# Sample attention by quads: four sequences per softmax tile, column tiles of 32, pages in two shared buffers

## The chip, the core and the metric

The kernel runs on one core of a Trainium2 chip. The time is the device time of one launch in microseconds (us), the median of several runs. Engines are named as the profile names them: PE (TensorE matmul), PEld (its weight load), DVE (VectorE), ACT (ScalarE), POOL (GpSimd), SP (SyncE, which here only issues DMAs and waits).

## What is computed

Two layers of a hybrid decoder, for a prompt of 1024 positions and for 8 short sample sequences of 4 positions each, 512 positions into their history. The change touches one part of layer 1, the sparse attention of the samples, whose keys and values lie in pages of 128 positions:

```python
def dsa_sample(q, k, v, qi, ki, wi, *, layer, cache_k, cache_v, cache_kidx, page_table):
    ...
    idx = index_select(qi, wi, ki_all, pos_q, k_sel)      # 129 of 516 keys per query
    ...
    ks = jnp.where(in_past, cache_k[layer, phys, off], k[nidx, nnew])
    vs = jnp.where(in_past, cache_v[layer, phys, off], v[nidx, nnew])
    return sparse_attend(q, ks, vs, idx, pos_q)

def sparse_attend(q, ks, vs, idx, pos_q):
    logits = jnp.einsum('nthd,ntkhd->nthk', q, ks).astype(jnp.float32) * ATT_SCALE
    ...
    p = jax.nn.softmax(jnp.where(valid, logits, -jnp.inf), axis=-1).astype(q.dtype)
    return jnp.einsum('nthk,ntkhd->nthd', p, vs)
```

The kernel does not gather keys. It computes the logits against all 512 paged keys and the 32 new ones (544 in all) and adds a large negative bias to those that were not chosen.

## The kernel before, in words

All dense work is a chain of 400 **slabs**. A slab is a block of a weight matrix with 128 output columns; SP loads it into one of three buffers (`load_slab`, which waits until the slab three places back has been multiplied), ACT writes its rounded part (L1064, `WH`), POOL the rest (L1531, `WL`), and PE multiplies 8 chunks of depth by three products each (L652, L653, L655). The result goes into one of two sets of PSUM banks, which ACT or DVE must empty before the slab after next may start (`evac_done`).

Every engine has its own hand-written program. It goes from slab to slab, and at the middle and at the end of each slab it calls its own `beside(n, end)`, which holds the side work due at that point. The engines run in program order, so side work that waits holds up all that stands behind it on its engine. F1A = 240 is the first slab of the stretch in question: the feed-forward part of layer 1 for the first half of the prompt (512 columns). Slabs 256 to 267 are up-projections in pairs (ACT copies the banks at L1204 and L1207, DVE does two convolution taps at L1823 and L1825 and, on the second of a pair, a product at L1949, after ACT's Silu at L1215). Slabs 268 to 275 are down-projections with 6 chunks of depth (DVE adds the banks to Z at L1864). Of the first two, PE computes four chunks each, then waits for the last `HLA` (L1937) of slab 267.

Beside these slabs run three things.

- Selection for the prompt, on DVE: at the end of each of slabs 256 to 271 three (in the last two: two) units of `best`, each a MAX8 pair (L2145) or a MATCH_REPLACE8 pair (L2143).
- A bisection for the last two prompt blocks, `threshold(k)` on DVE and `signs_of(k)` on ACT, in turns: DVE proposes a value (L2186 to L2191), ACT counts signs over 896 and 1024 columns (L1259), DVE takes the count and proposes the next. It has three steps per pair of up slabs and one per down slab.
- Sample attention, one sequence s for every two slabs. With a = n - 256: at the end of slab a = 2s PE computes `sample_logits(s)` (L843: four matmuls of 32 x 512 and four of 32 x 32, all float32; L844: the bias in bfloat16). DVE takes the row maximum (`sample_max`, L2252), ACT the exponential (L1271), DVE the reciprocal (`sample_recip`, L2257), ACT the scaling (L1276). At the end of slab a = 2s + 1 PE turns the probabilities (L853) and ACT copies them (`spt`, L1282 and L1283). At the end of slab a = 2s + 2 PE multiplies them by the values (`sample_values`, L864 and L865), and then does the logits of sequence s + 1. After each four sequences ACT keeps the sums (`kept`, L1288), PE turns them (L871), and ACT picks each head's own part (`atts`, L1295).

Keys have one buffer (`KP`), values another (`VP`). SP issues the four pages of a set one by one, each after reading its page number; the next keys once the logits of s are done, the next values once the value product of s is done. A set of either is 4 x 256 KB. From slab 275 on the same places hold the prompt's attention for its second half (logits at L896).

Of the kernel before, what the change touches and what calls it, by code (L numbers as in the profile page):

```python
# [22 lines left out]
I8 = mybir.dt.int8  # L23
# [142 lines left out]

def sample_at(n):

    a = n - F1A - S_FIRST
    return [[x // 2] if x % 2 == 0 and 0 <= x // 2 < SEQS else [] for x in (a - 1, a - 2, a)]  # L170

def kept_at(n):

    a = n - F1A - S_FIRST
    return [g for g in range(2) if a == 8 * g + 8], [g for g in range(2) if a == 8 * g + 9]
# [12 lines left out]
def build(nc, io):  # L189
    with ExitStack() as ctx:  # L190
# [53 lines left out]
        def piece(base, m):  # L244
# [87 lines left out]
            ("nmx", [P, 2], F32), ("psm", [P, 2], F32), ("prc", [P, 2], F32), ("rep", [NS, SEQS, NS], BF16),  # L332
# [20 lines left out]
        (spt, signs6), e = region(piece(z_off, 1), ("spt", [P, 5, NS], F32), ("signs6", [P, 7 * P], I8))  # L353
        assert e <= piece(z_off, 2)
        atts = at("atts", [P, 4, NS], F32, piece(z_off, 2))
# [4 lines left out]
        QBs = [at(f"QBs{c}", [P, SEQS, NS], F32, piece(z_off, 5 + c // 2) + c % 2 * SEQS * NS * 4) for c in range(4)]  # L360
# [84 lines left out]

        def dots_of(t):

            n = P * (3 + t // 8)
            return PS[:, (1, 3)[t % 2], 0:n] if t < 16 else pair(2 + t % 2, n)
# [8 lines left out]
        def attended_bank(p):  # L458
# [51 lines left out]
        k_in, v_in = sem("key_pages_in"), sem("value_pages_in")  # L510
        qb_zero, qb_set = sem("qb_cleared"), sem("qb_set")
        slg, smax, sexp, ssump, snorm, stp, ste, spv, satt = (
            sem("sa_" + n) for n in ("logits", "max", "exp", "rsum", "probs", "turned", "probs_turned", "values", "out"))
# [70 lines left out]
        def _(sp):  # L584
# [24 lines left out]
            def key_pages(s):  # L609
                for g in range(PAGES):  # L610
                    pg = page(s, g)
                    sp.dma_start(KP[:, :, HALF + g * PAGE:HALF + (g + 1) * PAGE],
                                 io["ck"][bass.ds(pg, 1)].rearrange("a p c s -> p (a c) s")).then_inc(k_in, 16)

            def value_pages(s):
                for g in range(PAGES):
                    pg = page(s, g)
                    sp.dma_start(VP[:, g, HALF:2 * HALF],
                                 io["cv"][bass.ds(pg, 1)].rearrange("a p c -> p (a c)")).then_inc(v_in, 16)

            for n in range(3, STEPS):
# [11 lines left out]
                if n == F1A + S_FIRST - 2:  # L633
# [3 lines left out]
                    value_pages(0)  # L637
# [10 lines left out]
        def _(pe):  # L648
# [180 lines left out]
            def sample_logits(s):  # L829
                if s == 0:  # L830
                    pe.wait_ge(qb_set, 8)
                    pe.wait_ge(sb_set, 2)
                    pe.wait_ge(rep_in, 16)
                    pe.wait_ge(ssc_set, 2)
                    pe.wait_ge(dot_relu, 48)
                else:
                    pe.wait_ge(sexp, s)
                pe.wait_ge(k_in, 64 * (s + 1))
# [8 lines left out]
            def sample_turn(s):  # L847
                pe.wait_ge(snorm, s + 1)
                if s >= 1:
                    pe.wait_ge(ste, 2 * s)  # L850
                for t in range(5):
                    w = P if t < 4 else NS
# [1654 lines left out]
```

## Time and profile before

| | us |
|---|---|
| median of 3 runs | 2792.41 |
| lowest, highest | 2786.95, 2792.7 |
| the profiled execution, its time | 2798.2 |
| its span, first to last instruction | 2796.5 |
| PE busy in the span | 2593.8 (93%) |
| DVE, ACT, POOL busy | 1479.6, 1264.8, 1213.7 |
| from the end of slab 256 (the first sample logits) to the first prompt logits of slab 275 | 1753.5 to 1967.9, that is 214.4 |

The last row is the stretch in which the sample attention runs. An engine's idle time is given with what ended it: [1.62 <-PE PS L844] behind a row means that the engine was idle for 1.62 us until the matmul of line 844 had finished.

### The profile page before, as it was taken

The page shows a single profiled execution, that of the slowest core. Times are in us where ns is not written, and L with a number is a line of the kernel's source. Part 1 is how long each engine was busy: PE and PEld are TensorE (multiplying, and loading weights), DVE is VectorE, ACT ScalarE, POOL GpSimd, SP SyncE. Part 2 cuts the span into 40 slices and gives each one's busy share as a digit, 9 for nine tenths or more (in the row PEclk, how much of TensorE's full clock was granted, in tenths as well). Part 3 has the DMA queues.
Part 4 walks back from the last instruction along what each step waited for, and adds up shares of the span by engine and source line. Part 5 has one row for each costly group of instructions (what it writes and reads, how often), then busy time and mean ns, then how long its engine had stood idle before and what let it go on. Part 6 is the DMA issues. An engine that isn't in the chain of part 4 may idle for free. (4 is left out here: it accounts for less than half of the span.)

```text
span 2796.5 us, 39511 instructions
## 1 busy us (share of the span) xinstructions
PE 2593.8 (93%) x15720; PEld 2221.3 (79%) x15720; DVE 1479.6 (53%) x2271; ACT 1264.8 (45%) x2019; POOL 1213.7 (43%) x1030
## 2 busy tenths in 40 slices
PE   7989999999999999999998976987999988999997
PEld 7989887888897788999987854543666667999997
DVE  2342476332574587634577488775553445542435
ACT  3111354343453444445443464673895734332333
POOL 2212455454464843434456664221332335454443
PEclk9999999999999999999999988998999998999998
DMA  3101222222313222222223313332212122222222
GB/s 127 43 32 46 84 90 83 91 94 95 98 63 110 83 76 68 69 76 69 89 91 119 110 59 115 110 123 91 68 57 89 57 89 84 84 87 87 84 94 80
DMA packets 96099, 235.45 MB, mean 84 GB/s; under 512 B 10443, under 2 KB 31499, under 8 KB 95531
## 3 DMA queue, kind: packets, MB, share of 16 engines
q1 hardware_dynamic: 85344, 210.95, 23.8%
q10 hardware_dynamic: 10570, 21.97, 2.2%
q8 instruction: 125, 2.05, 0.3%
q14 instruction: 60, 0.48, 0.1%
HBM read 219.43 MB, written 13.45 MB: 83 GB/s over the span
## 5 line engine op out<-in xcount | busy, mean ns | idle before, releaser
L1531 POOL TENSOR_TENSOR WL<-RAW,WH 128x1024 fp32r<-128x1024 f32 (+2 forms) x400 | 888.9, 2222 | 1479.7 <-ACT WH L1064 1479.2
L652 PE MATMUL PS<-XH,WH 128*128 128x272 f32 (+2 forms) x3312 | 1061.5, 331 | 38.1 <-DVE XL L1747 13.6
L653 PE MATMUL PS<-XL,WH 128*128 128x272 f32 (+2 forms) x3312 | 1045.3, 326 | 0.0
L655 PE MATMUL PS<-XH,WL 128*128 128x272 f32 (+2 forms) x3312 | 874.6, 326 | 0.0
L652 PEld LDWEIGHTS PS<-XH,WH 128*128 128x128 f32 x3312 | 630.7, 190 | 101.3 <-issue 39.0
L1064 ACT ACTIVATE WH<-RAW 128x1024 fp32r<-128x1024 f32 (+2 forms) x400 | 388.3, 971 | 611.9 <-DMA RAW<-in_slabs 593.7
L653 PEld LDWEIGHTS PS<-XL,WH 128*128 128x128 f32 x3312 | 630.5, 190 | 39.9 <-issue 1.0
L655 PEld LDWEIGHTS PS<-XH,WL 128*128 128x128 f32 x3312 | 561.6, 190 | 41.5
L652 PE MATMUL PS<-HH,WH 128*128 128x272 f32 (+1 forms) x880 | 265.2, 316 | 15.5 <-DVE HL L1937 13.8
L653 PE MATMUL PS<-HL,WH 128*128 128x272 f32 (+1 forms) x880 | 262.1, 312 | 0.0
L655 PE MATMUL PS<-HH,WL 128*128 128x272 f32 (+1 forms) x880 | 217.3, 312 | 0.0
L1864 DVE TENSOR_TENSOR Z<-Z,PS 128x512 f32<-128x512 f32 (+1 forms) x96 | 67.6, 704 | 236.8 <-PE PS L655 235.9
L652 PEld LDWEIGHTS PS<-HH,WH 128*128 128x128 f32 x880 | 168.5, 191 | 27.8 <-DVE HL L1937 14.9
L1823 DVE SCALAR_TENSOR_TENSOR cvB<-extB,fpar,cvB 128x560 f32<-128x560 f32 (+1 forms) x132 | 106.6, 808 | 149.5 <-ACT cvB L1207 146.4
L1816 DVE TENSOR_SCALAR cvB<-extB,fpar 128x560 f32<-128x560 f32 x88 | 54.3, 617 | 248.3 <-POOL extB L1650 178.9
L1204 ACT ACTIVATE extB<-PS 128x240 f32<-128x240 f32 (+3 forms) x308 | 92.1, 362 | 184.7 <-PE PS L655 184.7
L653 PEld LDWEIGHTS PS<-HL,WH 128*128 128x128 f32 x880 | 168.4, 191 | 8.0
L655 PEld LDWEIGHTS PS<-HH,WL 128*128 128x128 f32 x880 | 146.4, 191 | 7.5
L1823 DVE SCALAR_TENSOR_TENSOR cvA<-extA,fpar,cvA 128x512 f32<-128x512 f32 x44 | 58.3, 1324 | 129.2 <-ACT cvA L1207 127.4
L1825 DVE SCALAR_TENSOR_TENSOR cvB<-extB,fpar,cvB 128x560 f32<-128x560 f32 (+1 forms) x132 | 123.8, 938 | 4.7
L1575 POOL TENSOR_TENSOR Z<-Z,sqb 128x512 f32<-128x512 f32 (+1 forms) x64 | 98.2, 1551 | 14.2 <-ACT sqb L1133 14.2
L652 PE MATMUL PS<-HHA,WH 128*128 128x512 f32 x176 | 76.6, 435 | 27.3 <-DVE HLA L1937 15.6
(326 smaller groups left out, 3322.8 us busy)
## 6 DMA issues: line engine op xcount, KB each, us to landing
RAW<-in_slabs SPq DMA_DIRECT2D x272, 512.0 KB, 3.5
RAW<-in_slabs SPq DMA_DIRECT2D x96, 384.0 KB, 3.0
RAW<-in_slabs SPq DMA_DIRECT2D x32, 256.0 KB, 2.6
KP<-in_ck SPq DMA_DIRECT2D x32, 256.0 KB, 3.2
VP<-in_cv SPq DMA_DIRECT2D x32, 256.0 KB, 3.0
xb_rows<-spill ACTq DMA_DIRECT2D x8, 272.0 KB, 4.4
Z<-xb_rows ACTq DMA_DIRECT2D x1, 2176.0 KB, 9.2
out_o_y<-Z ACTq DMA_DIRECT2D x4, 544.0 KB, 2.8
```

The source lines that it names most:

```text
L652: pe.matmul(o, WH[n % 3][:, k, :], hi(k)[:, c], start=first, stop=False)
L653: pe.matmul(o, WH[n % 3][:, k, :], lo(k)[:, c], start=False, stop=False)
L655: mm = pe.matmul(o, WL[n % 3][:, k, :], hi(k)[:, c], start=False, stop=last)
L1064: act.activation(WH[n % 3][:, 0:kc, :], RAW[n % 3][:, 0:kc, :], ACT.Copy).then_inc(w_hi, 1)
L1204: ins = act.activation(dst, src_, ACT.Copy)
L1531: pool.tensor_tensor(WL[n % 3][:, 0:kc, :], RAW[n % 3][:, 0:kc, :], WH[n % 3][:, 0:kc, :].bitcast(F32), ALU.subtract).then_inc(w_lo, 1)
L1575: pool.tensor_tensor(z, z, LNS[q][3][:, :], ALU.subtract).then_inc(ln_sub, 1)
L1816: dve.tensor_scalar(out, row[:, 2:2 + w], taps_w[2], taps_w[3], ALU.mult, ALU.add).then_inc(tap_sem, 1)
L1823: dve.scalar_tensor_tensor(out, row[:, 0:w], taps_w[0], out, ALU.mult, ALU.add).then_inc(tap_sem, 1)
L1825: dve.scalar_tensor_tensor(out, row[:, 1:1 + w], taps_w[1], out, ALU.mult, ALU.add).then_inc(done, 1)
L1864: dve.tensor_tensor(by_bank(z, gr), by_bank(z, gr), slot(n), ALU.add).then_inc(evac_done[n % 2], 1)
```

## The change

The eight sequences form two quads, g = 0 and 1. In a quad the 128 rows of one softmax tile are 4 chunks of features (c, two heads each, 32 partitions) by 4 sequences (8 rows each).

- **Logits.** Sequence s comes at the end of slab a = s, one per slab. Chunk c multiplies only its own 32 partitions of the tile: four matmuls of 32 x 512 and four of 32 x 32 that write to partitions 0, 32, 64 and 96. The queries of a sequence stand in 8 of the 32 columns, the others are zero, so the four sequences of a quad add up in one pair of banks. The bias is added once for a quad, on all 128 partitions.
- **Softmax.** Maximum, exponential, reciprocal and scaling come once for a quad (slabs a = 3 and 7), on 128 x 544. They are turned at a = 4 and a = 11.
- **Values.** Sequence s comes at the end of slab a = 8 + s: 16 matmuls of 32 x 128 and 4 more for the new values, again in four column groups.
- **Pages.** `KP` and `VP` both serve keys and values; the set for step a + 2 is issued after step a.
- **`rep`**, the small matrix that spreads the bias, is loaded in 8 pieces instead of 1, on ACT's queue, at the point where the input projection of layer 1 begins (slab 128).

```diff
 def sample_at(n):
     a = n - F1A - S_FIRST
-    return [[x // 2] if x % 2 == 0 and 0 <= x // 2 < SEQS else [] for x in (a - 1, a - 2, a)]
+    return ([g for g in range(2) if a == (QUAD, 2 * SEQS - QUAD - 1)[g]], [a - SEQS] if SEQS <= a < 2 * SEQS else [],
+            [a] if 0 <= a < SEQS else [], [g for g in range(2) if a == QUAD * g + QUAD - 1])
...
                 a = n - 3 - F1A - S_FIRST
-                if a % 2 == 0 and 0 <= a // 2 < SEQS - 1:
-                    sp.wait_ge(slg, a // 2 + 1)
-                    key_pages(a // 2 + 1)
-                if a % 2 == 1 and 0 <= a // 2 - 1 < SEQS - 1:
-                    sp.wait_ge(spv, a // 2)
-                    value_pages(a // 2)
+                if 0 <= a < SEQS:
+                    sp.wait_ge(slg, a + 1)
+                    (key_pages if a + 2 < SEQS else value_pages)((a + 2) % SEQS)
+                elif SEQS <= a < 2 * SEQS - 2:
+                    sp.wait_ge(spv, a - SEQS + 1)
+                    value_pages(a - SEQS + 2)
...
             def sample_logits(s):
...
-                both = pair(3, SK, NS)
-                for o, keys, bias in ((both[:, 0:PAST], lambda c: KP[:, c, HALF:2 * HALF], sbias[:, 0:PAST]),
-                                      (both[:, PAST:SK], lambda c: K[:, c, NP:NT], sbias[:, PAST:SK])):
+                both = pair(3 - g, SK)
+                at0 = P * g + 24 * x
+                for cols in (slice(0, PAST), slice(PAST, SK)):
                     for c in range(4):
-                        pe.matmul(o, QBs[c][:, s, :], keys(c), start=(c == 0), stop=False)
-                    mm = pe.matmul(o, rep[:, s, :], bias, start=False, stop=True)
+                        keys = pages_of(s)[:, c, HALF:2 * HALF] if cols.start == 0 else K[:, c, NP:NT]
+                        mm = pe.matmul(both[32 * c:32 * c + 32, cols], QBs[c][:, at0:at0 + 32], keys, start=(x == 0), stop=False)
                 mm.then_inc(slg, 1)
+                if x == QUAD - 1:
+                    for cols in (slice(0, PAST), slice(PAST, SK)):
+                        mm = pe.matmul(both[:, cols], rep[:, g, :], sbias[:, cols], start=False, stop=True)
+                    mm.then_inc(sbiased, 1)
...
             def sample_values(s):
-                pe.wait_ge(ste, 2 * (s + 1))
-                pe.wait_ge(v_in, 64 * (s + 1))
...
+                pe.wait_ge(ste, 2 * (g + 1))
+                pe.wait_ge(page_in[s % 2], 64 * (s // 2 + 5))
                 for t in range(4):
-                    pe.matmul(o, spt[:, t, :], VP[:, t, HALF:2 * HALF], start=(t == 0), stop=False)
-                pe.matmul(o, spt[0:NS, 4, :], VS[:, :], start=False, stop=True).then_inc(spv, 1)
+                    for c in range(4):
+                        pe.matmul(sample_bank(g)[32 * c:32 * c + 32, x * P:(x + 1) * P], spt[:, t, 32 * c:32 * c + 32],
+                                  pages_of(s)[:, t, HALF + c * P:HALF + (c + 1) * P], start=(t == 0), stop=False)
...
-            def sample_max(s):
-                j = s % 2
-                dve.wait_ge(slg, s + 1)
-                dve.tensor_reduce(nmx[0:NS, j:j + 1], pair(3, SK, NS), AXX, ALU.max, negate=True).then_inc(smax, 1)
+            def sample_max(g):
+                dve.wait_ge(sbiased, g + 1)
+                dve.tensor_reduce(nmx[:, g:g + 1], pair(3 - g, SK), AXX, ALU.max, negate=True).then_inc(smax, 1)
```

On DVE, at the end of slab 258, before the change (cvA are the taps, HLA is the rest of the hidden row, SC the scores of the selection, tk the small values of the bisection):

```order
L1823 SCALAR_TENSOR_TENSOR cvA_159<-extA_157,fpar_178,cvA_159 128x512
L1825 SCALAR_TENSOR_TENSOR cvA_159<-extA_157,fpar_178,cvA_159 128x512
L1937 TENSOR_TENSOR HLA_153<-hfA,HHA_164 128x512
L2252 TENSOR_REDUCE nmx<-PS 32x1
L2257 RECIPROCAL prc<-psm 32x1
L2145 MAX m8a<-SC_149 128x8
L2145 MAX m8b<-SC_149 128x8
```

and after it:

```order
L1851 SCALAR_TENSOR_TENSOR cvA_159<-extA_157,fpar_178,cvA_159 128x512
L1853 SCALAR_TENSOR_TENSOR cvA_159<-extA_157,fpar_178,cvA_159 128x512
L1965 TENSOR_TENSOR HLA_153<-hfA,HHA_164 128x512
L2173 MAX m8a<-SC_149 128x8
L2173 MAX m8b<-SC_149 128x8
L2171 MATCH_REPLACE SC_149<-m8a,SC_149 128x640
```

The maximum and the reciprocal are gone from here; DVE's program now holds them twice (after L1977 of slabs 259 and 263, as 128x1) instead of eight times.

On PE, between slabs 258 and 259, before the change (VP, KP are the pages, QBs the queries, VS and K the new values and keys, rep and sbias the bias):

```order
L864 MATMUL PS<-VP,spt 32x512 x4
L865 MATMUL PS<-VS,spt 32x512
L843 MATMUL PS<-KP,QBs_214 32x512
L843 MATMUL PS<-KP,QBs_215 32x512
L843 MATMUL PS<-KP,QBs_216 32x512
L843 MATMUL PS<-KP,QBs_217 32x512
L844 MATMUL PS<-sbias,rep 32x512
L843 MATMUL PS<-K,QBs_214 32x32
```

After it, the logits between slabs 257 and 258, and the values between slabs 264 and 265:

```order
L860 MATMUL PS<-VP,QBs_215 32x512
L860 MATMUL PS<-VP,QBs_216 32x512
L860 MATMUL PS<-VP,QBs_217 32x512
L860 MATMUL PS<-VP,QBs_218 32x512
L860 MATMUL PS<-K,QBs_215 32x32
L860 MATMUL PS<-K,QBs_216 32x32
L860 MATMUL PS<-K,QBs_217 32x32
L860 MATMUL PS<-K,QBs_218 32x32
...
L881 MATMUL PS<-KP,spt 32x128 x16
L884 MATMUL PS<-VS,sptn 32x128 x4
```

A value product and a logits product no longer stand at the same place: the first eight slabs carry logits alone, the next eight values alone.

## Rows read from the trace of the kernel before

**Rows 1.** Busy time by stretch: length, PE, PEld, DVE, ACT, POOL, clock, DMA share, GB/s

```profile
1700.00:1753.00 53.00, 33.07 (x104) 24.39 (x105) 49.62 (x107) 24.45 (x38) 17.63 (x11) 0.77 0.44 142
1753.50:1967.90 214.40, 184.77 (x673) 97.90 (x673) 135.80 (x276) 129.55 (x225) 43.65 (x31) 0.93 0.35 109
1778.50:1803.10 24.60, 22.54 (x82) 11.69 (x81) 17.41 (x37) 16.80 (x28) 5.45 (x4) 0.93 0.41 128
```

**Rows 2.** Who waited for whom on DVE, 1753.5 to 1968: total, times, longest

```profile
DVE tk L2186 <- ACT signs L1259: 28.6, 8, 9.3
DVE nmx L2252 <- PE PS L844: 25.8, 6, 10.5
DVE cvA L1823 <- ACT cvA L1207: 9.0, 6, 1.5
DVE prc L2257 <- ACT sp L1271: 6.9, 8, 0.9
```

**Rows 3.** DVE in order of time, one pair of up slabs: start, duration, what

```profile
1783.00 0.71 DVE L2252 TENSOR_REDUCE nmx<-PS 32x1 f32<-32x544 f32 x1 [1.62 <-PE PS L844]
1784.58 0.15 DVE L2257 RECIPROCAL prc<-psm 32x1 f32<-32x1 f32 x1 [0.86 <-ACT sp L1271]
...
1789.55 0.13 DVE L2186 TENSOR_TENSOR tk<-tk 128x2 uint32<-128x2 f32 x1
...
1792.66 0.16 DVE L2186 TENSOR_TENSOR tk<-tk 128x2 uint32<-128x2 f32 x1 [2.58 <-ACT signs L1259]
...
1807.62 0.71 DVE L2252 TENSOR_REDUCE nmx<-PS 32x1 f32<-32x544 f32 x1 [1.61 <-PE PS L844]
```

**Rows 4.** PE in order of time, the sample work of one pair

```profile
1772.33 5.32 PE L864 MATMUL PS<-VP,spt 128*32 128x512 f32 x8 [2.45 <-ACT spt L1283]
1777.57 1.04 PE L865 MATMUL PS<-VS,spt 32*32 32x512 f32 x2
1778.54 3.62 PE L843 MATMUL PS<-KP,QBs 128*32 128x512 f32 x8
...
1782.41 0.44 PE L843 MATMUL PS<-K,QBs 128*32 128x32 f32 x8
...
1782.89 0.50 PE L652 MATMUL PS<-XH,WH 128*128 128x512 f32 x1
...
1788.66 0.46 PE L853 MATMUL PS<-ident,sp 32*128 32x32 f32 x5
```

**Rows 5.** DVE in order of time, slabs 271 and 272

```profile
1943.31 0.69 DVE L1864 TENSOR_TENSOR Z<-Z,PS 128x512 f32<-128x512 f32 x1
...
1947.22 2.05 DVE L2149 TENSOR_SCALAR MB<-SC 128x640 bf16<-128x640 f32 x2
1949.19 0.15 DVE L2186 TENSOR_TENSOR tk<-tk 128x2 uint32<-128x2 f32 x1
...
1959.87 0.16 DVE L2186 TENSOR_TENSOR tk<-tk 128x2 uint32<-128x2 f32 x1 [9.30 <-ACT signs L1259]
```

**Rows 6.** PE in order of time: prompt values, two column halves (128*64) side by side

```profile
2194.70 1.97 PE L927 MATMUL PS<-PTB,VT 128*64 128x128 f32 x32
```

**Rows 7.** All instructions on the value pages: duration min/median/max in ns, first and last start

```profile
L864 PEld LDWEIGHTS PS<-VP,spt x64: 106/111/178, 1772.3 to 1954.9; 128*32 128x32 f32 x64
```

**Rows 8.** The page, section 6: DMA issues, KB each, us to landing

```profile
RAW<-in_slabs SPq DMA_DIRECT2D x272, 512.0 KB, 3.5
...
KP<-in_ck SPq DMA_DIRECT2D x32, 256.0 KB, 3.2
```

**Rows 9.** SP's queue in order of time: one set of key pages

```profile
1783.71 4.46 SPq L612 DMA_DIRECT2D KP<-in_ck  x4
```

**Rows 10.** ACT and its DMA queue in order of time, around slab 128

```profile
852.93 0.45 ACTq L1489 DMA_DIRECT2D rep<-in_rep  x1
...
853.91 1.06 ACT L1064 ACTIVATE WH<-RAW 128x1024 fp32r<-128x1024 f32 x1 [2.97 <-DMA RAW<-in_slabs]
...
859.75 1.06 ACT L1064 ACTIVATE WH<-RAW 128x1024 fp32r<-128x1024 f32 x1 [2.84 <-DMA RAW<-in_slabs]
```

More of the change, by code:

```diff
@@ L359, in build @@
         signs = (signs6, signs7)
-        QBs = [at(f"QBs{c}", [P, SEQS, NS], F32, piece(z_off, 5 + c // 2) + c % 2 * SEQS * NS * 4) for c in range(4)]
+        QBs = [at(f"QBs{c}", [P, SEQS * NS], F32, piece(z_off, 5 + c // 2) + c % 2 * SEQS * NS * 4) for c in range(4)]
         PRB = at("PRB", [P, NP], F32, T0 - 4 * WID[1] * 4)
@@ L509, in build @@
         counted, proposed, small, placed = (sem("t_" + n) for n in ("counted", "proposed", "settled", "places"))
-        k_in, v_in = sem("key_pages_in"), sem("value_pages_in")
+        page_in = [sem("pages_in0"), sem("pages_in1")]
         qb_zero, qb_set = sem("qb_cleared"), sem("qb_set")
-        slg, smax, sexp, ssump, snorm, stp, ste, spv, satt = (
-            sem("sa_" + n) for n in ("logits", "max", "exp", "rsum", "probs", "turned", "probs_turned", "values", "out"))
+        slg, sbiased, smax, sexp, ssump, snorm, stp, ste, spv, satt = (
+            sem("sa_" + n) for n in ("logits", "biased", "max", "exp", "rsum", "probs", "turned", "probs_turned", "values", "out"))
         lg, amax, aexp, asum, anorm, atp, ate, apv, ao_hi, ao_lo = (
@@ L867, in sample_values_turn @@
             def sample_values_turn(g):
                 pe.wait_ge(sv_kept, g + 1)
-                for c in range(4):
-                    mm = pe.transpose(PS[:, 1, c * P:(c + 1) * P], kept[:, c * P:(c + 1) * P], ident[:, :])
+                own = ident[:, :].rearrange("p (c r) -> p c r", c=4)
+                for x in range(QUAD):
+                    mm = pe.matmul(sample_bank(g)[:, x * NS:(x + 1) * NS].rearrange("p (c r) -> p c r", c=4),
+                                   kept[:, x * P:(x + 1) * P], own[:, :, 8 * x:8 * x + 8], start=True, stop=True)
@@ L985, in beside @@
                 if end:
-                    late, out, now = sample_at(n)
-                    for s in late:
-                        sample_turn(s)
+                    late, out, now, _ = sample_at(n)
+                    for g in late:
+                        sample_turn(g)
                     for s in out:
@@ L1360, in beside @@
                 if end:
-                    late, out, now = sample_at(n)
-                    for s in late:
-                        sample_turned(s)
+                    late, _, _, full = sample_at(n)
+                    for g in late:
+                        sample_turned(g)
                     done, back = kept_at(n)
@@ L1368, in beside @@
                         sample_out(g)
-                    for s in now:
-                        sample_exp(s)
-                        sample_norm(s)
+                    for g in full:
+                        sample_exp(g)
+                        sample_norm(g)
                     for q in NORM_PLAIN:
@@ L1488, in _ @@
             act.dma_start(identb[:, :], io["identb"]).then_inc(identb_in, 16)
-            act.dma_start(rep[:, :, :], io["rep"]).then_inc(rep_in, 16)
+            for g in range(2):
+                for x in range(QUAD):
+                    act.dma_start(rep[:, g, :].rearrange("p (c s r) -> p c s r", c=4, s=QUAD)[:, :, x, :],
+                                  io["rep"][:, QUAD * g + x, :].rearrange("p (c r) -> p c r", c=4)).then_inc(rep_in, 16)
             act.dma_start(fpar1[:, :, :], io["fpar"][1]).then_inc(fpar_in, 16)
```

115 lines of the change are left out of this document (62 added, 53 removed).

## The prediction, made before the changed kernel was run

> **What bounds the kernel now.** I read the table of busy time by stretch first, then the waits of DVE, then the order of time. PE is 93% busy over the whole span, which says that most of the kernel is bound by it. The stretch of the sample attention is different. It lasts 214.4 us [rows 1], from the first sample logits to the first prompt logits of slab 275. PE is busy for 184.8 of it, but with the sample's own products, and it is not what the next step always waits for. DVE is busy for 135.8 and spends most of the rest in four waits [rows 2]: 28.6 for ACT's sign counts (the bisection, one after another by nature), 25.8 for the sample logits, 9.0 for ACT's copies, 6.9 for ACT's exponential. 135.8 + 70.3 = 206.1 of 214.4; the rest is small gaps. So DVE's program, its own work plus what it waits for in turn, accounts for the stretch, and I price the change on DVE first and ask afterwards whether PE keeps up.
>
> One pair of up slabs shows it [rows 3]. From one sample maximum to the next are 1807.62 - 1783.00 = 24.6 us. Of these the sample takes 1.61 (wait for the logits) + 0.71 (maximum) + 0.86 (wait for the exponential) + 0.15 (reciprocal) = 3.3. Everything else, 21.3, is selection (from the reciprocal to the next bisection step, 1784.73 to 1789.55, three units in 4.8), the bisection with a wait of 2.58, taps and the product. None of that changes.
>
> **Part 1, DVE's sample steps.** Removed: the wait for logits, 25.8 over six of the eight sequences; the wait for the exponential, 6.9; eight times 0.71 + 0.15, 6.9. Together 39.6 [rows 2, 3]. Added: two quads with the same steps, on 128 partitions instead of 32. I take the same durations, as the columns stay 544, and no wait for logits, as PE is far ahead there (part 3): 2 x (0.71 + 0.86 + 0.15) = 3.4. If the first exponential also had to wait for something of ACT, up to 2 us each more. Net -36.2.
>
> **Part 2, the end of the sample work.** At slab 272 DVE waits 9.30 for a sign count [rows 5], because ACT's program has the copy of the last value sums ahead of that count, and the value product came late. In an ordinary turn of the bisection that wait is 2.58 [rows 3]. With the last value product one slab earlier and a third as long, I expect the ordinary wait: -6.7. It could stay halfway if ACT's eight head copies fall there: -4.
>
> **Part 3, can PE keep up?** A slab of the up part takes 1788.66 - 1782.89 = 5.8, one of six chunks 4.3 [rows 4]. The sample work per sequence before: logits 1782.89 - 1778.54 = 4.35, turn 0.46, values 1778.54 - 1772.33 = 6.2 at a mixed clock.
> A float32 matmul appears as two records. Logits have the same 8 records of 512 columns (3.62 / 8 = 0.45 each) and 8 short ones (0.44 together). One after the other that is 4.1, four abreast 1.3. Values have 40 records of 128 columns, a quarter of 0.45 each, 0.11: 4.5 one after the other, 1.1 four abreast. No row shows four column tiles. The nearest shows two: 32 records in 1.97, 0.062 each instead of 0.11 [rows 6], which gives 2.5. I take 2.0 for either, nearer to that row than to the ideal.
> In the up slabs PE then needs 2 x (5.8 + 2.0) = 15.6 per pair, DVE 21.3. With no overlap at all it is 20.6, still covered. So the gain on DVE doesn't depend on the tiles running abreast there.
> In slabs 268 to 271 PE has less cover. DVE needs 0.69 + 4.8 + 0.5 = 6.0 for each of the first two; 3.9 + 0.5 = 4.4 for slab 270, which has two units; and 1949.19 - 1943.31 + 0.5 = 6.4 for 271 [rows 3, 5]: 22.8. PE needs 4 x (4.3 + 2.0) + 0.5 for the turn = 25.7. That gives back 2.9; with no overlap (4.5) it gives back 12.9, with four abreast nothing. I add 2 for low-clock stretches after PE's waits at the switch to the down slabs.
>
> **Part 4, ACT.** It loses six exponentials, scalings and turned copies. It was idle anyway (129.6 busy of 214.4 [rows 1]), so 0. If this shortens its side of the bisection it is a gain of a few tenths per pair, which I leave in the range.
>
> **Part 5, pages.** The 16 sets are the same bytes, now one set per slab instead of one. SP needs 4.46 to issue a set and a page lands 3.2 after that [rows 8, 9]: 7.7. The set is issued two slabs ahead of its use, 12.6 to 15.6 us. The slab load behind it on SP's queue waits for a slab to be multiplied; a slab with its sample work takes 6.3 or more, and SP's queue is held for 4.46 + 0.34, so the load isn't late. The share of DMA time rises from 0.35 [rows 1] to about 0.43. Cost 0, with up to 2 us per late set as the outer bound. The second set before the stretch now stands behind a slab load instead of ahead of it; DVE is busy 49.6 of 53.0 there [rows 1], so 0.
>
> **Part 6, `rep` in eight pieces.** Seven more issues of 0.45 on ACT, 3.2 us [rows 10]. ACT's slab work at 853.91 moves to 857.1; the next one, at 859.75, waits 2.84 for its own slab. ACT absorbs it, and PE has two slabs of lead: 0, at most +2.
>
> **Sum.** -39.6 + 3.4 - 6.7 + 2.9 + 2.0 = -38.0. The stretch becomes 176.4. The profiled execution would take 2798.2 - 38.0 = 2760.2; it lay 5.8 above the median, so for the median 2792.4 - 38.0 = **2754.4 us**.
>
> **Rivals.**
> **(a) The four column tiles run one after the other**, so the change does not do what "side by side" says. Logits 4.1, values 4.5. The up slabs hide it; the down slabs give back 12.9 instead of 2.9: 2764. A lower clock in those slabs does the same and worse, up to 2776. For: no row has four. Against: two tiles do overlap [rows 6].
> **(b) Each weight load waits for the product ahead of it.** A load takes 0.11 [rows 7]. Then values take 40 x 0.22 = 8.8 and logits 5.4. The down slabs need 4 x 13.1 + 0.5 = 52.9 against 22.8, 30.1 more; two up pairs with values 29.2 against 21.3, four with logits 22.4, together 20.2, less PE's lead of two slabs, 11.6. 38.7 in all in place of the 2.9: about 2790. Against: in rows 6 each of 32 records has its own load and takes 0.062, less than the load alone.
 If a share x of PE's time ran at half speed, a pair would need 15.6 (1 + x). It loses against DVE's 21.3 only from x = 0.37, and all parts together eat the gain at x = 0.65. At x = 0.8: pairs 28.1, 6 x 6.8 = 41 less the lead of 11.6; down slabs 45.6 against 22.8; the last four slabs +13: 65 instead of 4.9, about 2814. Against: where PE has no slack it is busy, and there the clock was 0.93 on average [rows 1].
> **(d) More than forecast**, down to 2740: four abreast, and ACT's lighter load shortens the bisection.
>
> **Chances.** Forecast (2744 to 2762) 0.62; (a) with clock 0.19; (d) 0.05; (b) 0.06; (c) 0.05; something unnamed near no change 0.03. The range from 2740 to 2776 takes in the forecast, (a) and (d). A measurement of this kernel tells about 0.2% from no change, 5.6 us. Faster than that 0.89, within it 0.06, slower 0.05.
>
> **What would show it.** Right: DVE has two waits for logits instead of eight, near 0 each; the time between DVE's steps of two pairs is 21 us; the wait of 9.3 is gone; PE waits for DVE or for the banks in slabs 257 to 267. Wrong: logits over 3 us or values over 4 us per sequence; PE waiting for pages; a clock below 0.8 in the down slabs; the part after slab 275 longer than before.

## The result, and the profile after

The changed kernel takes 2757.1 us, median of 4 runs (2752.3 to 2760.9), against 2792.6 for the kernel before beside it (2787.0 to 2793.6): 0.987 of its time, 95% interval 0.985 to 0.989, 35.5 us less. The profiled execution took 2760.7, its span is 2759.0. The four runs lie in two pairs, at 2752.3 and 2753.5 and at 2760.7 and 2760.9, so a difference of a few us from 2757.1 says little unless a trace shows it too.

Line numbers move: the slab products are now L667 to L670, the sample logits L860, their values L881 and L884, the bisection's comparison L2214, the maximum L2279, the reciprocal L2283, ACT's exponential L1295, POOL's split L1559.

Busy time by stretch (length, PE, PEld, DVE, ACT, POOL, clock, DMA share, GB/s), from the first sample logits to the first prompt logits, and the last part of it:

```profile
1758.10:1929.90 171.80, 130.25 (x878) 94.94 (x877) 132.61 (x263) 108.79 (x185) 43.24 (x31) 0.87 0.45 136
1902.60:1929.90 27.30, 27.30 (x195) 21.18 (x187) 21.55 (x48) 20.34 (x38) 10.52 (x6) 1.00 0.42 130
```

The stretch went from 214.4 [rows 1] to 171.8 us, 42.6 less. PE works 54.5 less in it, DVE 3.2 less: the busier one of the two was cut, and now they are level. In this execution the kernel reaches the stretch 4.5 us later than the kernel before does, so the spans differ by 37.5 only, and the medians by 35.5. Most of that comes from far ahead of anything that was changed, from a lower granted clock between 300 and 400 us. Same columns, the kernel before and then the changed one:

```profile
300.00:400.00 100.00, 95.95 (x612) 86.41 (x611) 66.29 (x84) 40.88 (x54) 50.76 (x27) 0.98 0.26 84
```

```profile
300.00:400.00 100.00, 95.90 (x592) 86.33 (x591) 68.05 (x83) 39.60 (x52) 50.92 (x27) 0.93 0.26 84
```

In the run with `rep` in one transfer, below, the clock there is 0.98 too, and it reaches the stretch at 1753.9.

Who waited for whom in the stretch (total, times, longest), DVE, then PE, then POOL and ACT:

```profile
DVE tk L2214 <- ACT signs L1283: 21.4, 9, 2.6
DVE cvA L1851 <- ACT cvA L1231: 9.0, 6, 1.5
DVE prc L2283 <- ACT sp L1295: 1.7, 2, 0.9
```

```profile
PE PS L667 <- POOL WL L1559: 25.3, 6, 8.4
PE PS L872 <- ACT sp L1299: 12.9, 1, 12.9
PE PS L667 <- DVE HLA L1965: 3.4, 1, 3.4
```

```profile
POOL WL L1559 <- ACT WH L1088: 133.5, 19, 13.8
ACT signs L1283 <- DVEq L2275: 46.1, 15, 5.3
```

Against [rows 2] the 25.8 for logits are gone, the longest wait for a count is 2.6 instead of 9.3, and the exponential is waited for twice. PE now waits for POOL's splits, which wait for ACT's rounding, which stands behind ACT's sign counts, which wait for DVE's proposals (L2275).

PE in order of time, logits and then values of one sequence:

```profile
1771.77 1.06 PE L860 MATMUL PS<-KP,QBs 128*32 128x512 f32 x8
1772.65 0.24 PE L860 MATMUL PS<-K,QBs 128*32 128x32 f32 x8
...
1833.38 1.08 PE L881 MATMUL PS<-KP,spt 128*32 128x128 f32 x32
1834.39 0.42 PE L884 MATMUL PS<-VS,sptn 32*32 32x128 f32 x8
```

Logits take 1.3 us instead of 4.3, values 1.5 instead of 6.2 [rows 4]. The 6.2 were at a mixed clock; a value product of the kernel before that ran at the full one took 4.5 (1846.33 to 1850.86).

DVE's bisection steps serve as marks. Until slab 268 the durations between them repeat with every pair of slabs: 3.1 between two steps of one slab, then one to the next slab's end, then one to the middle of the slab after. Before they were 3.1, 10.4, 11.1 (24.6 a pair, one pair of the five 22.9); after they are 3.1, 10.4, 7.7 (21.3) in three pairs of five and 3.1, 13.5, 7.7 (24.3) in the two with a quad's softmax. The table gives five such pairs, from slab 258 on, and the rest up to the first prompt logits, for every run below (each step is timed at its copy under a mask, on DVE in order of time):

| kernel | five pairs, us | rest, us | median, us |
|---|---|---|---|
| before | 121.4 | 81.4 | 2792.5 |
| after | 112.6 | 50.4 | 2757.1 |
| softmax later, in the kernel before | 119.0 | 82.7 | 2792.4 |
| four groups, in the kernel before | 114.7 | 66.7 | 2770.5 |
| one group | 112.8 | 63.2 | 2768.7 |
| one buffer per kind | 112.7 | 62.9 | 2767.3 |
| quads alone (both) | 122.3 | 77.6 | 2792.9 |
| extra maximum | 116.9 | 48.1 | 2760.1 |
| quad's softmax later | 117.7 | 48.1 | 2757.4 |
| rep in one transfer | 112.6 | 51.9 | 2756.3 |
| fewer units in the up slabs | 107.3 | 53.7 | 2755.7 |
| units early and late | 99.0 | 53.1 | 2746.7 |
| units done by slab 273 | 99.0 | 52.7 | **2746.2** |
| more units early | 95.1 | 52.5 | 2750.6 |

Most of the gain, 31.0, lies in the rest; the pairs gave 8.8, and 2.8 the steps ahead of the first mark. Busy time in the rest, same columns as above, before and then after:

```profile
1886.50:1967.90 81.40, 64.19 (x216) 33.06 (x214) 38.11 (x83) 37.01 (x70) 14.45 (x9) 0.87 0.30 92
```

```profile
1879.50:1929.90 50.40, 41.44 (x299) 31.48 (x299) 36.81 (x79) 33.82 (x67) 14.74 (x9) 0.86 0.33 100
```

DVE's work in it is 1.3 less, PE's 22.8. The kernel before has three value and two logits products there, the changed one four of values.

### The profile page after: what moved, and what is told of

The parts are those of the page before. It is cut to its first block, busy times and chain, and to the rows that moved or that the text cites. A ratio compares the mean times of both kernels' runs of the same rounds, so it can differ in the third digit from the quotient of the medians.

```text
span 2759.0 us, 39856 instructions
## 1 busy us (share of the span) xinstructions
PE 2538.9 (92%) x15926; PEld 2219.2 (80%) x15926; DVE 1487.2 (54%) x2259; ACT 1245.5 (45%) x1981; POOL 1220.2 (44%) x1030
## 4 chain that ended last, share of the span: by engine, by line
PE 68%; DVE 16%; ACT 7%; issue 4%; DMA 2%; POOL 1%; ACTq 0%; SPq 0%; DVEq 0%; POOLq 0%
PE PS L667 21%; PE PS L668 20%; PE PS L670 20%; DMA RAW<-in_slabs 2%; DVE SC L2171 2%; POOL WL L1559 1%; PE PS L920 1%; ACT WH L1088 1%; DVE cvB L1853 1%; DVE cvB L1851 1%; DVE cvA L1851 1%; PE PS L951 1%; PE PS L839 1%; DVE m8b L2173 1%; PE PS L936 1%
## 5 line engine op out<-in xcount | busy, mean ns | idle before, releaser
L1559 POOL TENSOR_TENSOR WL<-RAW,WH 128x1024 fp32r<-128x1024 f32 (+2 forms) x400 | 889.8, 2225 | 1438.1 <-ACT WH L1088 1437.9
L667 PE MATMUL PS<-XH,WH 128*128 128x272 f32 (+2 forms) x3312 | 1064.7, 332 | 58.4 <-POOL WL L1559 22.1
L670 PE MATMUL PS<-XH,WL 128*128 128x272 f32 (+2 forms) x3312 | 875.7, 326 | 0.0
L667 PEld LDWEIGHTS PS<-XH,WH 128*128 128x128 f32 x3312 | 631.9, 191 | 123.1 <-issue 41.5
L670 PEld LDWEIGHTS PS<-XH,WL 128*128 128x128 f32 x3312 | 562.6, 191 | 42.0
L667 PE MATMUL PS<-HH,WH 128*128 128x272 f32 (+1 forms) x880 | 265.0, 316 | 16.5 <-DVE HL L1965 14.2
L670 PE MATMUL PS<-HH,WL 128*128 128x272 f32 (+1 forms) x880 | 216.8, 312 | 0.0
L1851 DVE SCALAR_TENSOR_TENSOR cvB<-extB,fpar,cvB 128x560 f32<-128x560 f32 (+1 forms) x132 | 112.6, 853 | 149.4 <-ACT cvB L1231 146.3
L667 PEld LDWEIGHTS PS<-HH,WH 128*128 128x128 f32 x880 | 168.3, 191 | 28.9 <-DVE HL L1965 15.3
L670 PEld LDWEIGHTS PS<-HH,WL 128*128 128x128 f32 x880 | 146.1, 191 | 7.4
L667 PE MATMUL PS<-HHA,WH 128*128 128x512 f32 x176 | 75.5, 429 | 32.6 <-DVE HLA L1965 15.8
```

The costliest lines, as they stand in the source:

```text
L667: pe.matmul(o, WH[n % 3][:, k, :], hi(k)[:, c], start=first, stop=False)
L670: mm = pe.matmul(o, WL[n % 3][:, k, :], hi(k)[:, c], start=False, stop=last)
L1559: pool.tensor_tensor(WL[n % 3][:, 0:kc, :], RAW[n % 3][:, 0:kc, :], WH[n % 3][:, 0:kc, :].bitcast(F32), ALU.subtract).then_inc(w_lo, 1)
L1851: dve.scalar_tensor_tensor(out, row[:, 0:w], taps_w[0], out, ALU.mult, ALU.add).then_inc(tap_sem, 1)
```

## Experiments

My theory at first was the prediction's: DVE sets the up slabs, its wait for logits was the loss, and PE matters in the down slabs alone. The rival: PE's saved work is the gain.

**One group of columns.** The products of all chunks go to group 0, so they can't run abreast; the bias goes to each group by itself. The attention of three chunks in four is left out, the matmuls of keys and values keep their number and shapes.

```diff
-mm = pe.matmul(both[32 * c:32 * c + 32, cols], QBs[c][:, at0:at0 + 32], keys, start=(x == 0), stop=False)
+mm = pe.matmul(both[0:32, cols], QBs[c][:, at0:at0 + 32], keys, start=(x == 0 and c == 0), stop=False)
...
-pe.matmul(sample_bank(g)[32 * c:32 * c + 32, x * P:(x + 1) * P], spt[:, t, 32 * c:32 * c + 32], ...
+pe.matmul(sample_bank(g)[0:32, x * P:(x + 1) * P], spt[:, t, 32 * c:32 * c + 32], ...
```

> The changed kernel with all four chunks' products of a sequence on one group of 32 columns instead of four, the number of matmuls and their shapes the same (the bias goes to the other three groups alone, and the attention of three chunks in four is lost, so the sample outputs are not those of the reference). With one group the products can't run beside each other: logits 8 x 0.45 + 0.44 = 4.1 us instead of 1.3, values 40 x 0.11 = 4.5 instead of 1.5. Theory (DVE's program sets the up slabs, PE only the down slabs): nothing in the up slabs, where PE is idle for 20 to 40 us; in the four down slabs with values 4 x 3.0 = 12, so 2757 + 12 = 2769. Rival (PE's saved time is the gain): 8 x (2.8 + 3.0) = 46 more, 2803, as slow as before or slower. Rival (the products ran beside each other for another reason than the groups): no change, 2757.

2768.7 (2766.5 to 2773.8), 11.5 us more, 0.992 of before (0.990 to 0.993). PE in order of time, the first logits and one set of values:

```profile
1754.41 3.59 PE L860 MATMUL PS<-KP,QBs 128*32 128x512 f32 x8 [0.17 <-issue]
...
1846.27 3.68 PE L882 MATMUL PS<-VP,spt 128*32 128x128 f32 x32
```

So the groups are what makes them run abreast: 1.06 against 3.59 for eight records, 1.08 against 3.68 for 32. The five pairs are untouched (112.8), the rest is 12.8 longer: as the theory says, and in a kernel that has two page buffers (see "quads alone").

**Softmax later, in the kernel before.** If DVE's wait for logits is the loss, it is enough to let DVE come later.

```diff
 # DVE, at the end of a slab
-for s in sample_at(n)[2]:
-    sample_max(s)
-    sample_recip(s)
 ...
 if (n, end) in STEP_AT:
     threshold(STEP_AT[n, end])
+if end:
+    for s in sample_at(n)[2]:
+        sample_max(s)
+        sample_recip(s)
 # ACT: sample_exp and sample_norm likewise, behind signs_of(k)
```

> The kernel before with one thing moved: DVE's maximum and reciprocal of a sequence stand behind the bisection step of the same slab end instead of ahead of the selection units (some 5 us later), and ACT's exponential behind the sign counts. No quads, no column groups, pages as before. Theory (a large part of the gain is DVE's 25.8 us wait for logits): the wait is gone, 2792.5 - 20 to 25 = 2770, less what PE's turn then waits for the probabilities. Rival (the gain is PE's saved work): PE's work is unchanged, so no change, 2792.

2792.4 (2789.2 to 2794.5), ratio 0.9998 (0.9988 to 1.0008): no change. Waits of DVE and then of PE in that kernel, 1753 to 1968:

```profile
DVE tk L2187 <- ACT signs L1259: 32.8, 9, 9.8
DVE nmx L2253 <- PE PS L844: 15.7, 2, 11.2
...
DVE Z L1865 <- PE PS L655: 5.2, 3, 2.7
```

```profile
PE PS L853 <- ACT sp L1276: 12.4, 7, 2.8
PE PS L864 <- DMA VP<-in_cv: 10.1, 3, 5.9
```

The wait for logits is left in two places, where it is long, and others have grown (counts 28.6 to 32.8, the add of a product 2.6 to 5.2). PE waits more (12.4 instead of 1.0 for the scaled probabilities). In the five pairs 2.4 us were won, and 1.3 lost again in the rest. My theory fell on this run: of the 25.8 us at most what lay in the up slabs, 1.6 a pair, was DVE's to gain; elsewhere the wait only showed that PE was late.
Following the chain of work back through one pair of up slabs of the kernel before (start, duration) shows what the 1.6 belonged to:

```profile
1783.00 0.72 DVE nmx L2252
...
1786.30 1.72 DVE SC L2143 x2
...
1791.21 1.41 ACT signs L1259 x3
...
1796.57 0.26 ACT spt L1282
...
1796.95 5.32 PE PS L864 x8
```

It is a ring: PE's values and logits (10.7 of the 24.6), then DVE's maximum, with ACT's exponential, its selection units and proposal (7.2), then ACT's sign counts, rounding, bank copies and at last `spt` (6.8), for which the next values wait [rows 4]. In two of the five pairs PE's wait ends otherwise, once with a value page and once with `atts`. No engine alone set these slabs. The ring gets shorter when the maximum comes later (pairs of 23.7 here) or when PE's products do ("four groups", below, 22.9), down to what DVE needs by itself, 21.3 and 1.7.

**Extra maximum.** One more reduction per slab, eight in all.

```diff
+for s in sample_at(n)[2]:
+    dve.tensor_reduce(s8[:, s:s + 1], ssc[:, :], AXX, ALU.max)
 for g in sample_at(n)[3]:
     sample_max(g)
```

> The changed kernel with one more reduction of 32 x 544 float32 on DVE at the end of each of the eight slabs with sample logits; its result is not used. Theory (DVE sets the up slabs): 8 x 0.7 = 5.6 us longer, 2763; each bisection step of slabs 258 to 265 comes 0.7 later per slab. Rival (PE or ACT sets them): no change, 2757.

2760.1 (2757.9 to 2765.0): 3.0 more, an interval that reaches from none to the expected 5.6. The trace is plainer: the durations are 11.0 and 8.3 instead of 10.4 and 7.7, 0.6 for each reduction, and five pairs, which hold seven of the eight, take 4.3 more. DVE does set the up slabs of the changed kernel. Then 2.3 come back. Same columns as the first table of stretches, the slab behind the last up slab in this kernel and in the changed one:

```profile
1893.00:1901.90 8.90, 7.45 (x103) 5.49 (x104) 6.78 (x14) 3.88 (x13) 0.00 (x0) 1.00 0.44 129
```

```profile
1892.10:1902.60 10.50, 9.05 (x97) 6.53 (x97) 6.79 (x15) 3.92 (x13) 0.00 (x0) 0.67 0.44 123
```

The same work takes 8.9 us at a clock of 1.00 and 10.5 at 0.67. In both PE idles much ahead of it; what decides which of them meets the low level there I can't tell from these runs.

**One buffer per kind.** Keys go to `KP`, values to `VP`, and a set is issued when the one before it has been used.

```diff
-    sp.wait_ge(slg, a + 1)
-    (key_pages if a + 2 < SEQS else value_pages)((a + 2) % SEQS)
+    sp.wait_ge(slg, a + 1)
+    key_pages(a + 1)
...
-    sp.wait_ge(spv, a - SEQS + 1)
-    value_pages(a - SEQS + 2)
+    sp.wait_ge(spv, a - SEQS + 1)
+    value_pages(a - SEQS + 1)
```

> The changed kernel with the page buffers as before: all key sets go to one, all value sets to the other, and a set is issued only when its predecessor has been used; one set per slab as in the changed kernel. A set needs 4.46 us of issue and 3.2 to land, 7.7. Theory: an up slab takes 11.4 us, so nothing there; from the first down slab on, where a slab takes 4.3 + 1.5 = 5.8, PE waits about 3 to 4 us for each of three value sets, and SP's slab loads stand behind them: 2757 + 11 = 2768. Rival (the second buffer is not needed, the pages are hidden anyway): 2757.

2767.3 (2762.8 to 2772.6), 10.2 more. PE's waits for pages:

```profile
PE PS L856 <- DMA KP<-in_ck: 11.6, 6, 2.5
PE PS L877 <- DMA VP<-in_cv: 10.4, 4, 4.9
```

The 11.6 for keys lie where PE has slack and cost nothing (112.7 for five pairs); the rest is 12.5 longer, with 9.6 of the waits for values in it. In the changed kernel PE doesn't wait for pages at all.

**Four groups, in the kernel before**, without quads. The sums of the four chunks are not put together; each product has the size of the changed kernel's.

```diff
-    for c in range(4):
-        pe.matmul(o, QBs[c][:, s, :], keys(c), start=(c == 0), stop=False)
+    for c in (1, 2, 3, 0):
+        pe.matmul(o(c), QBs[c][:, s, :], keys(c), start=True, stop=(c > 0))
...
-    pe.matmul(o, spt[:, t, :], VP[:, t, HALF:2 * HALF], start=(t == 0), stop=False)
+    for c in range(4):
+        pe.matmul(o(c), spt[:, t, :], VP[:, t, HALF + c * P:HALF + (c + 1) * P], start=(t == 0), stop=False)
```

> The kernel before with column groups alone: each chunk's logits and values of a sequence go to a group of 32 columns of its own, four abreast, values as 128-wide products; softmax per sequence, pages and schedule as before. The chunks' sums are not put together, so the sample attention is wrong, but each product has the size of the changed kernel. Theory after the first four runs (in the down slabs PE's own work and its wait for value pages set the pace, in the up slabs DVE): up pairs 24.6 - 1.6 = 23.0, five pairs, some 7 us; in the down slabs 3 to 4 sequences each 7.0 us of PE shorter, part of which goes into a longer wait for value pages (12.3 us now): 10 to 20 us. 2792.5 - 17 to 27 = 2766 to 2776. Rival (the gain needs the two softmax tiles): under 7 us, 2786 or more.

2770.5 (2767.6 to 2775.6), 0.993 of before (0.992 to 0.995): 21 of the 35 us, with one softmax per sequence. The pairs have 3.1, 10.4, 9.4: DVE's 21.3 and a softmax of 1.7, as expected, and no wait for logits in them. What holds PE now:

```profile
PE PS L866 <- ACT spt L1287: 17.7, 4, 5.2
PE PS L866 <- DMA VP<-in_cv: 9.4, 2, 6.0
```

**Quads alone**: the edits of "one group" and "one buffer per kind" together.

> The changed kernel with both of its other parts undone: all products of a sequence on one group of columns (the attention of three chunks in four is lost) and one page buffer per kind. What is left are the two softmax tiles, the schedule of eight logits and then eight values, and the values in 128-wide products. One part undone alone cost 11.5 (groups) and 10.2 us (buffers). Theory (in a down slab the page set, 7.7 us behind the last use, comes on top of the products that use it, 4.5): 12.2 a slab instead of 8.8 with two buffers, three times, so 10 on top of the 11.5: 2779, and the quads alone are worth about 14. Rival (the waits overlap, the longer product hides the pages): 2769.

2792.9 (2789.5 to 2796.0), ratio 1.0004 (0.9994 to 1.0013). All of the gain is gone, where I expected 22 of 36 us to go. All of PE's waits in the stretch but one of 0.2, and the chain followed back from 1875 to 1765, share of each line:

```profile
PE PS L856 <- DMA KP<-in_ck: 15.7, 7, 2.7
PE PS L878 <- DMA VP<-in_cv: 15.1, 6, 5.1
```

```profile
by line: PE PS L856 30.7%; DMA KP<-in_ck 21.5%; SPq L612 12.9%; SPq L623 10.4%; issue 8.0%; PE PS L878 6.6%; DMA VP<-in_cv 5.3%; SPq L629 2.4%; PE PS L663 1.9%; PE PS L881 1.8%; PE PS L666 1.7%; PE PS L664 1.7%; PE PS L861 0.3%
```

PE waits for no other engine, and the chain holds its products (L856 are the logits), the reading of page numbers and issuing of pages on SP (L612, L623, L629) and their landing, nothing of DVE or ACT. In the changed kernel the same view (it cuts the line off) is the reverse, DVE's program with ACT's counts and copies:

```profile
by line: DVE SC L2171 22.8%; DVE cvA L1851 11.7%; DVE m8b L2173 10.9%; DVE m8a L2173 10.0%; issue 7.2%; ACT signs L1283 6.6%; DVE cvA L1853 6.2%; ACT WH L1088 4.1%; DVE tk L2214 3.4%; DVE hfA L1977 3.1%; ACT cvA L1231 3.1%; DVE HLA L1965 2.
```

With that the four kernels with quads read as one rule:

| | two shared buffers | one per kind |
|---|---|---|
| four groups | 2757.1 | 2767.3 |
| one group | 2768.7 | 2792.9 |

Either part takes 24 to 26 us off 2792.9, the other one then 10 to 12 more. Each part of the stretch is as long as the longer of two paths, PE's with its pages and DVE's with its counts. The table of marks says where the second cut is lost. In the five pairs either cut alone brings PE's path below DVE's (122.3 to 112.8 or 112.7), and the other adds nothing (112.6). In the rest, where PE is the longer one, both count: 77.6, then 63.2 or 62.9, then 50.4.

**rep in one transfer.**

```diff
-for g in range(2):
-    for x in range(QUAD):
-        act.dma_start(rep[:, g, :].rearrange(...)[:, :, x, :], io["rep"][:, QUAD * g + x, :]...).then_inc(rep_in, 16)
+act.dma_start(rep[:, :, :], io["rep"]).then_inc(rep_in, 16)
```

> The changed kernel with the array rep laid out by the host in the order of its tile and loaded by one transfer instead of eight. Theory (seven more issues of 0.6 us on ACT are hidden): 2757, no change, though ACT's slab work after them comes 4 us earlier. Rival (they delay PE, the 5 us by which the changed kernel's trace lies behind at slab 140): 2752.

2756.3 (2753.8 to 2758.3): no change that can be told. In the changed kernel, on ACT and its queue in order of time:

```profile
857.80 4.79 ACTq L1516 DMA_DIRECT2D rep<-in_rep  x8
...
863.12 1.06 ACT L1088 ACTIVATE WH<-RAW 128x1024 fp32r<-128x1024 f32 x1 [7.30 <-issue]
```

ACT's next slab comes after 7.30 us of issuing, 4.79 of them for `rep`, and what reaches PE at the next product, at 866.71, is a wait of 0.21.

The 5 us by which that trace was behind aren't caused by the eight transfers: the median doesn't change, and the changed kernel is 4.9 behind the kernel before as soon as the first of them is issued (857.80 against 852.93 [rows 10]).

**Quad's softmax later**, in the changed kernel; the edit is that of "softmax later".

> The changed kernel with a quad's maximum and reciprocal on DVE behind the bisection step of its slab end, and its exponential on ACT behind the sign counts. In the changed kernel the three durations between bisection steps are 3.1, 10.4, 7.7 us in a pair of up slabs without a quad and 3.1, 13.5, 7.7 in one with: 3.1 more, of which 1.7 are the softmax steps and 1.5 a two-column comparison that takes 1.65 instead of 0.15 while POOL runs a split. Theory (DVE's first operation on two SBUF operands waits while POOL's split holds their common access, and whether it meets it is a matter of timing): the comparison takes 0.15 in these two pairs, a quad costs 1.7 to 2.5, the time is 1 to 3 us less, 2755. Rival (the 1.5 belong to the quad whatever the timing): 3.1 as before, 2757.

It rests on this row of the changed kernel, DVE and POOL in order of time:

```profile
1802.41 2.41 POOL L1559 TENSOR_TENSOR WL<-RAW,WH 128x1024 fp32r<-128x1024 f32 x1 [7.36 <-ACT WH L1088]
...
1803.19 1.65 DVE L2214 TENSOR_TENSOR tk<-tk 128x2 uint32<-128x2 f32 x1
```

A comparison of two columns takes 1.65 us and ends when POOL's split does (1804.8); elsewhere it takes 0.15. Moved, it takes 0.15 in both quads. But the time is 2757.4 (2756.0 to 2761.8), and a quad costs 5.7 instead of 3.1. DVE and POOL of this kernel:

```profile
1798.66 0.72 DVE L2280 TENSOR_REDUCE nmx<-PS 128x1 f32<-128x544 f32 x1
...
1802.23 2.36 POOL L1560 TENSOR_TENSOR WL<-RAW,WH 128x1024 fp32r<-128x1024 f32 x1 [10.75 <-ACT WH L1088]
1803.34 1.80 DVE L1852 SCALAR_TENSOR_TENSOR cvA<-extA,fpar,cvA 128x512 f32<-128x512 f32 x1 [2.92 <-ACT cvA L1231]
```

The split now holds a convolution tap (1.80 instead of 0.75), and DVE waits 2.92 for ACT, which does the exponential ahead of its copies: 1.7 + 2.9 + 1.05 = 5.7. So whom the split meets is timing, as the theory says; the gain I expected of it isn't there.
The Trainium skill (SBUF — State Buffer, "SBUF: two separate sides") says that a DVE operation with two SBUF inputs and a GpSimd operation that reads SBUF exclude each other for a whole instruction. These rows agree, down to an operation of two columns.

**Moving DVE's work.** If DVE sets the up slabs and PE the rest, selection units should leave the up slabs. Only the table of units per slab changes:

```diff
-TOP45 = dict(zip(list(range(F1A + 2, F1A + 8)) + list(range(F1A + 16, F1A + 32)), [3] * 20 + [2] * 2))
+# fewer in the up slabs: range(F1A + 16, F1A + 34), [3] * 6 + [3, 2] * 6 + [3, 3, 3, 3, 2, 2]
+# early and late:        range(F1A + 16, F1A + 34), [4] * 5 + [3] + [2] * 12 + [3, 3, 3, 3, 3, 2]
+# done by slab 273:      range(F1A + 16, F1A + 33), [4] * 6 + [2] * 12 + [4, 3, 3, 3, 3]
+# more early:            range(F1A + 16, F1A + 33), [5, 5, 5, 5, 4, 4] + [2, 2, 1] * 4 + [4, 3, 3, 3, 3]
```

> The changed kernel with six of DVE's selection units moved: 3 and 2 in turn instead of 3 in each of slabs 257 to 268, and 3, 3, 3, 3, 2, 2 in slabs 269 to 274 instead of 3, 3, 2, 2. Theory (DVE sets the up slabs, PE the down slabs): 6 x 1.6 = 9.6 us off the up slabs, pairs of 19.7 instead of 21.3, and 1 to 3 given back in slabs 271 to 274: 2750. Rival (PE's clock or POOL's splits set the up slabs now): no change, 2757.

2755.7 (2752.3 to 2759.3), 1.4 less where 7 were expected; too little to tell from no change. Pairs without a quad are 19.7 to 20.6 (19.7 expected), but five take only 5.3 less, since a quad's pair is still 23.5. The rest takes 3.3 more, of which this wait is 3.1:

```profile
PE PS L920 <- DVE MB L2177: 3.1, 1, 3.1
```

> As the run before it, and five more units moved ahead, to slabs 243 to 247, where DVE is busy for 17 to 20 of 30 us: 4 instead of 3 in each, 2 in each up slab, 3, 3, 3, 3, 3, 2 in slabs 269 to 274. Theory (DVE sets the up slabs): 12 x 1.6 = 19 us off them, pairs of 18.1, up to 5 given back at both ends: 2742 to 2747. Rival (PE, which needs 14.1 of a pair at full clock, is slowed by its idle time and takes over): 2750 as the run before.

2746.7 (2746.5 to 2747.5), 10.4 less, 0.984 of before (0.982 to 0.986). Pairs without a quad are 17.9 to 18.9, with one 21.9.

> The run with units early and late, which took 2746.7 us, with the last of them one slab sooner: 4 units in each of slabs 243 to 248, 2 in each up slab, 4, 3, 3, 3, 3 in slabs 269 to 273, none in 274. In that run PE waited 3.1 us for the bias tile that follows DVE's last unit. Theory (that wait is the late unit's): the wait gone, pairs in the up slabs unchanged, 2744. Rival (DVE sets slabs 269 to 274 as a whole, so the work only moves inside them): 2747, and a wait as long elsewhere.

2746.2 (2746.1 to 2746.4), the best version. The wait for the bias tile is gone, yet the time is the same within 0.5: that fits the rival, by which DVE's work only moved within these slabs. Where the 3.1 us went isn't shown; PE's waits for DVE's adds grew by 1.1.

> The run with the units done by slab 273, which took 2746.2 us, with four more units moved ahead of the sample work: 5, 5, 5, 5, 4, 4 in slabs 243 to 248 (DVE was busy for 42 of 60 us there), 2, 2, 1 in turn in the up slabs. Theory (DVE still sets the up slabs: pairs of 17.9 against PE's 14.1): 4 x 1.6 = 6.4 us off them, up to 3 given back ahead: 2740 to 2743. Rival (PE, ACT or POOL now set one of the two stretches): 2746.

2750.6 (2748.3 to 2752.3), 4.3 slower than the best. The pairs gain 3.9, but the first sample logits come 5.1 later (1760.2 instead of 1755.1). The longest wait of PE ahead of them, 1580 to 1755, in the best version and then here:

```profile
PE PS L808 <- DVE ra L2131: 13.2, 1, 13.2
```

```profile
PE PS L808 <- DVE ra L2131: 18.8, 1, 18.8
```

There PE's second four sequences of index products wait for DVE to rectify the first four, and this step stands behind the early units on DVE: 5.6 longer, about what the logits come later. DVE's busy share ahead, 42 of 60 us, had suggested room, but it was read from 1590 to 1650, and the early units begin at 1642.9: from 1650 to 1710, where they stand, DVE was busy for 55.4 of 60 in the best version.

## Why the prediction was right, and where its reasons were not

The time of 2757.1 lies 2.7 above the forecast of 2754.4; the stretch fell to 171.8 where 176.4 was said. The single steps did less well than the sum.

**What bounds the kernel now: wrong, and the root of the rest.** I added DVE's work and its waits, 206 of 214.4, and concluded that DVE's program accounts for the stretch. That sum comes out for any engine: PE's 184.8 and its waits of 29.7 make 214.5. It says nothing about who is ahead. What does is who waits for whom. DVE waited 25.8 for PE [rows 2]; PE waited directly for DVE only 3.2, and 12.3 for value pages, in the same trace, waits of PE, 1753.5 to 1967.9:

```profile
PE PS L864 <- DMA VP<-in_cv: 12.3, 3, 6.0
PE PS L864 <- ACT spt L1283: 6.6, 3, 2.5
PE PS L864 <- ACT atts L1295: 3.2, 1, 3.2
...
PE PS L652 <- DVE HLA L1937: 3.2, 1, 3.2
```

The prediction doesn't use this view. In the rest, where most of the gain lies, the bound was PE's path with its value pages: with that path as it was, the kernel's time didn't move for a later softmax, nor for two softmax tiles instead of eight ("softmax later", "quads alone"), and shorter products alone won 21 us ("four groups"). In the up slabs it was the ring of the three engines, which a later maximum cut as well as shorter products did.

**Part 1, DVE's steps: right in size per pair, wrong in place.** A pair without a quad is 21.3, as forecast. But five pairs gave 8.8, not 5 x 3.3 - 3.4 = 13.1: one of the old pairs took 22.9 and not 24.6, and each quad costs 3.1 instead of 1.7, as POOL's split holds the comparison. In the down slabs the removed waits were a symptom. DVE's waits for the two quads' logits are 0, as said.

**Part 2, the wait of 9.30: right that it goes.** The longest is 2.6, and the last two of the stretch are 1.75. That it was worth 6.7 by itself isn't shown: it hung on a value product for which PE had waited 3.9 for its pages, so it was part of PE's lateness too.

**Part 3, PE keeps up: the products mis-sized, in the safe direction.** I took 2.0 us for logits and for values; they take 1.3 and 1.5. The ideal, 1.3 and 1.1, was nearer than the row with two tiles [rows 6]. So the 2.9 given back didn't come about. In the up slabs PE waits, as said, but for POOL's splits and the scaled probabilities, not for DVE directly. "The gain doesn't depend on the tiles running abreast" holds for the up slabs (112.8 with one group), and for the whole it is 11.5 of 35.5 us as long as the buffers are shared; with one buffer per kind it is 25.6. The 2.0 for a low clock at the switch to the down slabs has about the size of that slab's loss, 10.5 at 0.67 against 8.9 at 1.00. That slab is also the forecast's own sign of being wrong, a clock below 0.8 in the down slabs; over the whole rest the clock is 0.86, and it was 0.87 before.

**Part 4, ACT: 0 fits, the reason doesn't.** DVE's waits for ACT's copies are 9.0 as before. "Idle anyway" overlooks that ACT's part was 6.8 us of the ring's 24.6. **Part 6, `rep`: right** at 0.

**Part 5, pages: the cost right, the gain missed.** The new order costs nothing, and the share of DMA time is 0.45 where 0.43 was said. But I looked only for what the new order might cost, and not for what the old one did. The 12.3 us of PE's waits for value pages went, and two shared buffers are worth 10.2 us here, 24.2 without the groups.

So two errors met: a gain booked to DVE that was mostly PE's, and one from the pages that wasn't booked. That the sum came within 2.7 us is in part luck.

(c), the clock, did less: it fell from 0.93 to 0.87 over the stretch, and was 1.00 from 1902.6 on. (d) names what happened, abreast in full, though it wasn't enough to leave the forecast.

## What to carry to other kernels

The busy time and the waits of an engine add up to the stretch for every engine, bound or not; read the waits of both sides and see who waits for whom before a wait is booked as a gain, and follow the chain back through one period: it can go around several engines, and then no one of them is the bound. Where two paths run beside each other, price a change as the longer one's new length, part by part: once the other path is the longer one, a second cut is worth nothing there, and a cut on the shorter path never was. When the bound has moved to another engine, look for that engine's work that can go to slabs where it has slack: here a table of numbers gave 10.9 us more, until a step that waited behind the moved work became late.

## What the runs showed of the hardware

- Four products that differ in the group of 32 output columns run 3.4 times as fast as on one group (1.06 against 3.59 us for 8 records of 512 columns, 1.08 against 3.68 for 32 of 128), though each has its own weight load of 0.11.
- A DVE operation of two columns took 1.65 us instead of 0.15 while POOL ran a split on SBUF.
- Eight small loads (2 KB each) hold ACT's queue for 4.79 us, 0.45 each but for one of 1.4.
- Two runs with the same PE instructions behind an idle PE met clocks of 0.67 and 1.00, 1.6 us apart over one slab. What decides it stays open. It also stays open why, far ahead of the change, one execution had 0.93 and others 0.98 between 300 and 400 us.
